# Where the softmax's normalisation runs, and how the first branch's keys are made

## The chip, the cores and the metric

The kernel runs on one core of one Trainium2 chip. The metric is the device time of one execution in microseconds (us); lower is better. TensorE (PE), VectorE (DVE), ScalarE (ACT), GpSimd (POOL) and SyncE (SP, which starts the weight transfers) each run their own instruction list in order, and wait for one another by semaphores. "PEld" in the profile is TensorE's loading of stationary operands, which overlaps its matmuls.

## The reference, cut to what matters

Two layers of a block with three attention branches over 512 image tokens (x) and 256 context tokens (c), width 1024, one batch. In each layer the normalised and modulated tokens `h` are projected by one wide matrix `w_in`. The first branch (`mla`) has 8 heads of 64 + 32 rotary dimensions, whose keys and values come from a 256-wide latent and whose queries come from a 384-wide latent; the rotary part of the key is shared by all heads. The second (`swa`) looks at a window of 128 tokens on either side and at the context, with a sink logit; the third (`ax`) is dense with normalised keys and queries.

```python
ckv, kr, sk, sv, ak, av = _split(p, KV_SPLITS)
kv_m = (rmsnorm(ckv, lw['mla_kv_norm']) @ lw['mla_w_ukv']).reshape(B, T, 8, 64 + 64)
k_m = concatenate([kv_m[..., :64], broadcast_to(k_rope, (B, T, 8, 32))], axis=-1)
q_m = (rmsnorm(cq, lw['mla_q_norm']) @ lw['mla_w_uq']).reshape(B, T, 8, 1, 64 + 32)
s = einsum('bqhgd,bkhd->bhgqk', q, k) * scale      # each branch
p = softmax(s);  o = einsum('bhgqk,bkhd->bqhgd', p, v)
y_b = (o_b * silu(z_b)) @ w_o_b;   y = sum_b sigmoid(g_b) * y_b;   x = x + gate * (y @ w_out)
```

In the first layer the context tokens are updated too (they have queries); in the second only the image tokens are.

## The kernel before, in words

**Precision.** Every fp32 operand of a large matmul is held as two reduced parts, high and low (`_hi`, `_lo`), and a product is three matmuls: high by high, high by low, low by high. Weights arrive by DMA in chunks of up to 128x1024 in one of a few slots; ScalarE makes the high part (`w_hi`, line 1355) and GpSimd the low one (`w_lo`, line 1528).

**Attention units.** A unit is one head by one tile of 128 query tokens; there are 48 per branch in the first layer (8 heads by 6 tiles), 32 in the second, 240 in all. Two units of one head make a pass. For each unit the function `attention` writes out, in this order, the events of every engine:

- PV: TensorE multiplies the probabilities transposed in the iteration before by the values (lines 1224 and 1225).
- T: TensorE transposes blocks of normalised exponentials `e` into `ptp` (line 1211); ScalarE copies them out as the high part (1445). They belong to a pass whose last unit is at least two units back, and TensorE waits for that unit's normalisation (`norm_done`, in the branch `ev == "T"` of TensorE's list).
- SB: TensorE's last scores of this unit into `wide` (1195), after waiting for the exponential of the unit before.
- N: VectorE normalises the exponentials of the unit *before*: a reciprocal of the sum (1731), then a multiplication of the whole 128 x width tile by it, in place (1732). The two are chained by a semaphore.
- X: VectorE's row maximum over the scores (1715) and the bias from it (1721, in `swa` 1718).
- OC, TL, O: ScalarE copies half of a finished pass's output (1454); VectorE makes the low part of the transposed probabilities (1737), adds the output's halves (1744) and gates them (1750).
- M: ScalarE's exponential with accumulated sum (1436).
- SA: TensorE's first scores of the next unit, and after it `fill`: steps of other work (projections of later heads and branches, gates, output projections) from a queue.

`fill` gives every unit an equal share of the work still listed for the branch, by the planner's costs; a credit that finds no eligible work is cut to 900 ns. Items marked urgent come first once their condition holds. The items of the first branch are `mla_head(1)` to `mla_head(7)`, the first table, keys and queries of the second branch, two gate tiles (`z`) and `values_s` (the values of the second and third branches, three groups of 48 matmuls of 256 columns, line 677).

**First branch's heads.** `mla_head(h)` (line 595) makes the keys of head h (`km`, 64 rows, six matmuls for x and six for c), on even h the values of two heads (`vm`), and the queries of head h+1 (`qm`); head 0 makes the queries of heads 0 and 1. A head's work may start when head h-2 has been issued, since `k_m` has two buffers. The rotary rows of the keys (`kr`) are written into both buffers once a layer. The weights of one `mla_head` form one chunk `mk`.

**Memory.** `k_m` is two buffers in one tensor; `v_s` (values of the later branches) lies at offset 12288 to 24576 of the shared area, `lat_r` and `ak_sq` at 18432 and 21504.

Of the kernel before, what the change touches and what calls it, by code (L numbers as in the profile page):

```python
# [122 lines left out]
def schedule():  # L123
# [416 lines left out]
    for l in range(LAYERS):  # L540
# [52 lines left out]
        first_q = {0: (0, 1), 7: ()}  # L593

        def mla_head(h):

            qs = first_q.get(h, (h + 1,))
            c = chunk("mk", l, h, qs)
            kg = [project("km", l, c, tg, src="ckv", m=MLA_NOPE, width=MLA_NOPE, k=KKV, needs=lambda: latents, what="km", head=h)
                  for tg in ("x", "c")]  # L600
            ready.setdefault(("mla", h), []).extend(kg)
            vg = []
            if h % 2 == 0:
                vg = [group("vm", chunk_ids=(c,), mode="vm", l=l, cost=cost_of(128, 6 * 3), co=KKV * MLA_NOPE,
                            tts=range(tt, tt + 3), what="vm", pair=h // 2, needs=lambda: latents) for tt in range(0, TT, 3)]
                ready_v["mla", h // 2] = vg
            qg, co = [], KKV * (MLA_NOPE + 2 * MLA_V * (h % 2 == 0))
            for i, hq in enumerate(qs):
                got = [project("qm", l, c, tg, src="cq", co=co + i * KQ * MLA_K, m=MLA_K, width=MLA_K, k=KQ,
                               needs=lambda: latents, what="qm", head=hq, **roped(tg)) for tg in tgs]  # L610
                ready.setdefault(("mla", hq), []).extend(got)
                qg += got
            return [s for g in (qg + kg + vg if h == 0 else kg + qg + vg) for s in g["steps"]]
# [32 lines left out]
        def q_pair(branch, t):  # L646
            def make():
                c = chunk("win", l, C_Q[branch] + t * P, P)
                gs = [project("qs", l, c, tg, what="qs", head=2 * t, branch=branch,
                              kx=keys[branch][0]["low_n"], **roped(tg, squares=branch == "ax")) for tg in tgs]  # L650
# [18 lines left out]
        for h in range(1, HEADS):  # L669
            cost = cost_of(SEQ, 9 + 6) + cost_of(CTX, 6 + 9 * (len(tgs) > 1)) + (2 * cost_of(128, 18) if h % 2 == 0 else 0)  # L670
            item(("mla", h), "mla", cost, lambda s, h=h: h < 2 or ("mla", h - 2) in s, lambda h=h: mla_head(h), urgent=True)
# [5 lines left out]
        item("values_s", "mla", 3 * cost_of(256, 48), lambda s: True, values_s)  # L677
# [70 lines left out]
def build(nc, t_in, out):  # L748
# [62 lines left out]
    k_m = shared("k_m", [P, 2, 2, TOK], R, 63488)  # L811
# [44 lines left out]
    with ExitStack() as stack:  # L856
# [26 lines left out]
        s_done, max_done, exp_done, norm_done = (semaphore(k) for k in ("s_done", "max_done", "exp_done", "norm_done"))  # L883
        pt_done, pt_hi_ready, pt_lo_ready = semaphore("pt_done"), semaphore("pt_hi_ready"), semaphore("pt_lo_ready")
# [24 lines left out]
        def f(ap):  # L909
            return ap.bitcast(F)  # L910


        def chunk_dma(c):
# [18 lines left out]
            if kind == "mk":  # L932
                h, qs = chunks[c][2:]
                got, at = [], KKV * MLA_NOPE
                got.append((raw[:, 0:at].rearrange("p (k c) -> p k c", k=KKV),
                            t_in["mla_w_ukv"][l, :, h * P:h * P + MLA_NOPE].rearrange("(k p) c -> p k c", p=P)))
                if h % 2 == 0:
                    for k in range(KKV):
                        rows = t_in["mla_w_ukv"][l, k * P:(k + 1) * P, h * P:(h + 2) * P].rearrange("p (h a d) -> p h a d", h=2, a=2)
                        got.append((raw[:, at:at + 2 * MLA_V].rearrange("p (h d) -> p h d", h=2), rows[:, :, 1, :]))  # L940
                        at += 2 * MLA_V
                for hq in qs:
                    got.append((raw[:, at:at + KQ * MLA_K].rearrange("p (k c) -> p k c", k=KQ),
                                t_in["mla_w_uq"][l, :, hq * MLA_K:(hq + 1) * MLA_K].rearrange("(k p) c -> p k c", p=P)))
                    at += KQ * MLA_K
                return got
# [5 lines left out]
        def chunk_size(c):  # L952
            kind = chunks[c][0]
            if kind == "win":
                return KD * chunks[c][3]
            if kind == "mk":
                h, qs = chunks[c][2:]
                return KKV * (MLA_NOPE + 2 * MLA_V * (h % 2 == 0)) + KQ * MLA_K * len(qs)
            return KO * P if kind == "wo" else CHUNK
# [38 lines left out]

        def q_of(u):
            cs_ = slice(u["tt"] * P, (u["tt"] + 1) * P)  # L1000
            if u["branch"] == "mla":
                return [q_m[u["h"] % 3][0:MLA_K, i, cs_] for i in range(2)]
            return [q_s[:, u["h"] % 4, cs_]]

        def k_of(u, k0, nk):
            if u["branch"] == "mla":
                return [k_m[0:MLA_K, u["h"] % 2, i, k0:k0 + nk] for i in range(2)]
            return [k_s[:, u["h"] // (HEADS // KVH), i, k0:k0 + nk] for i in range(2)]
# [100 lines left out]
        def _(pe):  # L1109
# [11 lines left out]
            for e in events:  # L1121
# [78 lines left out]
                elif ev == "T":  # L1200
                    t = e["t"]
                    if new(norm_done, t["pa"]["units"][-1]["n"] + 1):
                        pe.wait_ge(norm_done, t["pa"]["units"][-1]["n"] + 1)
# [39 lines left out]
        def pieces(g):  # L1243
# [13 lines left out]
            if what == "km":  # L1257
                s = g["head"] % 2
                return [(k_m[0:MLA_NOPE, s, 0, c], k_m[0:MLA_NOPE, s, 1, c], src[0:MLA_NOPE, 0:N])], None
            if what == "kr":  # L1260
                rows = slice(MLA_NOPE, MLA_K)
                s = src[rows, 0:N] if g["roped"] else src[0:MLA_ROPE, 0:N]
                return [(k_m[rows, i, 0, c], k_m[rows, i, 1, c], s) for i in range(2)], None
# [70 lines left out]
        def _(act):  # L1334
# [13 lines left out]
            for e in events:  # L1348
# [73 lines left out]
                elif ev == "M":  # L1422
# [10 lines left out]
                    else:  # L1433
# [3 lines left out]
                                         bias=nbias[:, r:r + 1], scale=scale, accum_out=esum[:, r:r + 1]).then_inc(exp_done, 1)  # L1437
                elif ev == "T":
# [60 lines left out]
                elif ev == "XM":  # L1499
# [4 lines left out]
                    nc.scalar.activation(h_hi[:, :, tt * P:(tt + 1) * P], m, ACT.Copy).then_inc(x_h, 1)  # L1504
                elif ev == "XS":
# [64 lines left out]
        def _(dve):  # L1570
# [30 lines left out]
            for e in events:  # L1601
# [120 lines left out]
                elif ev == "N":  # L1722
# [128 lines left out]
```

## Time and profile before

| what | us |
|---|---|
| three runs | 2092.71, 2095.66, 2084.99 (median 2092.71) |
| the profiled execution: its own time | 2090.13 |
| its span in the trace | 2088.3 |
| mean granted TensorE clock | 0.947 of full speed |

The page gives each engine's busy time, the costliest groups of instructions and the chain of work that ended last. In the trace, the first layer attends from about 213 to 945 us and the second from about 1350 to 1935 us; the branches follow one another, `mla`, `swa`, `ax`, with borders near 450 and 690, and near 1535 and 1730. Before, between and after lie the modulation, the latent projections and the merge and output projections. A matmul's duration in the profile is longer than the distance between two of them, because they are pipelined; distances are read from start to start. The chain of waits is followed back only to about 1280 us, so it describes the second layer's attention and end.

### The profile page before, as it was taken

The numbers are of one execution on the slowest core, as the hardware profiler recorded it, in microseconds if no ns is written. First come the engines' busy times: TensorE is split into PE (matmuls) and PEld (weight loads), VectorE is DVE, ScalarE is ACT, GpSimd is POOL, SyncE is SP. The second block draws the span as 40 slices with busy tenths as digits, with TensorE's granted clock in tenths as the row PEclk, the third lists the DMA queues.
The fourth block names the chain that finished last, engine by engine and source line by source line (L and its number), as shares of the span: only waits on it lengthen the run. The fifth ranks groups of instructions, "written<-read, shape, count | busy, mean of one in ns | idle before, by whom it ended". The sixth has DMA issues, their size and how long they took to land. (4 is left out here: it accounts for less than half of the span.)

```text
span 2088.3 us, 27530 instructions
## 1 busy us (share of the span) xinstructions
PE 1822.0 (87%) x10845; PEld 1560.1 (75%) x10845; DVE 1216.3 (58%) x2322; ACT 902.2 (43%) x1691; POOL 604.3 (29%) x328
## 2 busy tenths in 40 slices
PE   5598999879999899998888978888879988999887
PEld 2376778768998788887766966777767876878667
DVE  1524775786666677765232354376867677677324
ACT  1323554544554555544222143344545455554332
POOL 0332221212221222213455153221213323332551
PEclk9699999999999999999998989899989999999999
DMA  6220010101121111113334212110102221111442
GB/s 221 58 58 20 22 32 19 41 11 41 46 56 41 32 40 46 31 42 115 107 113 144 62 61 63 35 28 23 41 16 62 63 64 45 52 52 50 136 141 81
DMA packets 192287, 125.90 MB, mean 60 GB/s; under 512 B 21468, under 2 KB 187934, under 8 KB 192158
## 3 DMA queue, kind: packets, MB, share of 16 engines
q1 hardware_dynamic: 187248, 108.57, 18.3%
q10 hardware_dynamic: 3630, 11.37, 1.5%
q0 software_dynamic: 1280, 4.20, 0.6%
q8 instruction: 86, 1.41, 0.3%
q14 instruction: 43, 0.35, 0.1%
HBM read 119.92 MB, written 4.19 MB: 59 GB/s over the span
## 5 line engine op out<-in xcount | busy, mean ns | idle before, releaser
L1528 POOL TENSOR_TENSOR w_lo<-w_raw,w_hi 128x1024 fp32r<-128x1024 f32 (+6 forms) x220 | 464.4, 2119 | 1181.1 <-ACT w_hi L1355 1181.0
L1172 PE MATMUL acc<-h_hi,w_hi 128*128 128x512 f32 (+2 forms) x1288 | 471.2, 366 | 48.8 <-POOL w_lo L1528 24.4
L1172 PE MATMUL acc<-h_hi,w_lo 128*128 128x512 f32 (+2 forms) x1288 | 466.3, 362 | 0.0
L1172 PE MATMUL acc<-h_lo,w_hi 128*128 128x512 f32 (+2 forms) x1288 | 461.0, 360 | 0.0
L1172 PEld LDWEIGHTS acc<-h_hi,w_hi 128*128 128x128 f32 (+1 forms) x1288 | 248.9, 193 | 91.2 <-issue 27.1
L1445 ACT ACTIVATE pt<-ptp 128x512 fp32r<-128x512 f32 (+3 forms) x312 | 166.2, 563 | 280.1 <-PE ptp L1211 279.3
L1172 PEld LDWEIGHTS acc<-h_hi,w_lo 128*128 128x128 f32 (+1 forms) x1288 | 248.3, 193 | 36.6
L1172 PEld LDWEIGHTS acc<-h_lo,w_hi 128*128 128x128 f32 (+1 forms) x1288 | 246.0, 191 | 36.7
L1715 DVE TENSOR_REDUCE nmax<-wide 128x1 f32<-128x768 f32 (+3 forms) x240 | 190.5, 794 | 112.0 <-PE wide L1195 110.5
L1355 ACT ACTIVATE w_hi<-w_raw 128x1024 fp32r<-128x1024 f32 (+6 forms) x220 | 200.0, 921 | 79.6 <-DMA w_raw<-in_w_out 68.2
L1436 ACT ACTIVATE e<-wide,nbias,rq 128x768 f32<-128x768 f32 x160 | 145.1, 907 | 182.6 <-DVE nbias L1721 182.1
L1737 DVE TENSOR_TENSOR pt<-ptp,pt 128x512 fp32r<-128x512 f32 (+3 forms) x312 | 192.1, 641 | 40.2 <-ACT pt L1445 40.2
L1732 DVE TENSOR_SCALAR e<-e,einv 128x768 f32<-128x768 f32 (+3 forms) x240 | 176.3, 735 | 8.5
L1211 PE MATMUL ptp<-ident,e 128*128 128x128 f32 x1152 | 168.5, 281 | 0.0
L1195 PE MATMUL wide<-k_s,q_s 128*128 128x256 f32 (+2 forms) x576 | 128.1, 340 | 16.9 <-DVE q_s L1313 11.1
L1211 PEld LDWEIGHTS ptp<-ident,e 128*128 128x128 f32 x1152 | 136.5, 145 | 1.4
L1224 PE MATMUL pv<-pt,v_s 128*128 128x256 f32 (+1 forms) x384 | 100.8, 289 | 36.9 <-DVE pt L1737 22.5
L1224 PEld LDWEIGHTS pv<-pt,v_s 128*128 128x128 f32 x384 | 73.1, 190 | 52.0 <-DVE pt L1737 47.4
L1670 DVE SCALAR_TENSOR_TENSOR th_x<-th_x,acc 128x512 f32<-128x512 f32 x32 | 22.0, 686 | 153.4 <-PE acc L1172 153.2
L1172 PE MATMUL acc<-og_hi,w_hi 128*128 128x512 f32 (+1 forms) x288 | 103.8, 360 | 5.2 <-ACT th_x L1395 4.9
L1554 POOL TENSOR_TENSOR swapped<-swapped,sin 128x512 f32<-128x512 f32 (+2 forms) x38 | 49.8, 1309 | 188.5 <-DVE rot L1628 171.8
L1172 PE MATMUL acc<-og_hi,w_lo 128*128 128x512 f32 (+1 forms) x288 | 103.5, 360 | 0.0
(192 smaller groups left out, 3377.6 us busy)
## 6 DMA issues: line engine op xcount, KB each, us to landing
w_raw<-in_w_in SPq DMA_DIRECT2D x102, 512.0 KB, 3.8
w_raw<-in_ada_w SPq DMA_DIRECT2D x48, 512.0 KB, 3.8
w_raw<-in_w_out SPq DMA_DIRECT2D x16, 512.0 KB, 4.0
xres<-in_x ACTq DMA_DIRECT2D x2, 2048.0 KB, 9.1
w_raw<-in_w_o_mla SPq DMA_DIRECT2D x16, 256.0 KB, 2.8
w_raw<-in_w_o_swa SPq DMA_DIRECT2D x16, 256.0 KB, 2.8
w_raw<-in_w_o_ax SPq DMA_DIRECT2D x16, 256.0 KB, 2.8
w_raw<-in_mla_w_uq SPq DMA_DIRECT2D x16, 144.0 KB, 2.4
```

What stands on the lines that cost most here:

```text
L1172: ins = nc.tensor.matmul(dst, lhs, rhs, start=first, stop=last)
L1195: ins = nc.tensor.matmul(wide[:, c0:c0 + nk], lhs, rhs, start=(i == 0), stop=(i == len(pairs) - 1 and not masks))
L1211: ins = nc.tensor.transpose(ptp_of(t)[:, b:b + P], e_of(u, c0, c0 + P), ident[:, :])
L1224: nc.tensor.matmul(dst, v_of(pa, kt), pt_of(t, 0)[:, b], start=t["first"] and i == 0, stop=False)
L1355: nc.scalar.activation(w_hi[s][:, 0:k], w_raw[s][:, 0:k], ACT.Copy).then_inc(w_hi_ready, 1)
L1436: nc.scalar.activation(e_of(u), wide[:, u["lo"]:u["lo"] + u["width"]], ACT.Exp, bias=nbias[:, r:r + 1], scale=scale, accum_out=esum[:, r:r ...
L1445: nc.scalar.activation(pt_of(t, 0), ptp_of(t), ACT.Copy).then_inc(pt_hi_ready, 1)
L1528: nc.gpsimd.tensor_tensor(w_lo[s][:, 0:k], w_raw[s][:, 0:k], f(w_hi[s][:, 0:k]), ALU.subtract).then_inc(w_lo_ready, 1)
L1554: nc.gpsimd.tensor_tensor(swapped[rows, :], swapped[rows, :], sin[rows, :], ALU.mult).then_inc(rope_link, 1)
L1715: link(nc.vector.tensor_reduce(nmax[:, r:r + 1], wide[:, u["lo"]:u["lo"] + u["width"]], AX.X, ALU.max, negate=True))
L1732: nc.vector.tensor_scalar(e_of(u), e_of(u), einv[:, r:r + 1], None, ALU.mult).then_inc(norm_done, 1)
L1737: nc.vector.tensor_tensor(pt_of(t, 1), ptp_of(t), f(pt_of(t, 0)), ALU.subtract).then_inc(pt_lo_ready, 1)
```

## The change

Two parts.

1. The multiplication of N moves from VectorE to ScalarE for all three branches (`on_act = BRANCHES`): VectorE keeps the reciprocal, which signals `inv_done`; ScalarE waits for it, scales `e` in place (a Copy with a per-partition scale) and signals `norm_act`, for which the transposes wait. In ScalarE's list this stands where the event N stands: behind the copies of T, ahead of OC and of the exponential M.
2. The keys of two heads are made by one projection of 128 rows (`m` and `width` at their default 128), on even h, with a chunk `mk` that holds the keys and values of two heads and one head's queries; the other heads' queries have a chunk `mq` of their own. Odd `mla_head` makes queries only, head 7 nothing. `k_m` becomes three buffers; the third lies at 18432 and its rotary rows are copied by ScalarE once a layer (event KC, after a wait for all low parts). Since it overlaps `v_s`, `values_s` may start only when head 5 has been issued.

```diff
+        emit("KC", l_done=n["l"])
+
+        def head_q(h, c, co):
+            got = [project("qm", l, c, tg, src="cq", co=co, m=MLA_K, width=MLA_K, k=KQ,
+                           needs=lambda: latents, what="qm", head=h, **roped(tg)) for tg in tgs]
+            ready.setdefault(("mla", h), []).extend(got)
+            return got
 
         def mla_head(h):
-            qs = first_q.get(h, (h + 1,))
-            c = chunk("mk", l, h, qs)
-            kg = [project("km", l, c, tg, src="ckv", m=MLA_NOPE, width=MLA_NOPE, k=KKV, needs=lambda: latents, what="km", head=h)
-                  for tg in ("x", "c")]
...
+            kg, vg, qg = [], [], []
             if h % 2 == 0:
+                c = chunk("mk", l, h, h + 1 if h else 0)
+                kg = [project("km", l, c, tg, src="ckv", k=KKV, needs=lambda: latents, what="km", head=h) for tg in ("x", "c")]
+                for hk in (h, h + 1):
+                    ready.setdefault(("mla", hk), []).extend(kg)
...
+                qg = head_q(h + 1 if h else 0, c, KKV * 2 * (MLA_NOPE + MLA_V))
+            if h == 0 or h % 2 and h + 1 < HEADS:
+                qg += head_q(h + 1, chunk("mq", l, h + 1), 0)
             return [s for g in (qg + kg + vg if h == 0 else kg + qg + vg) for s in g["steps"]]
...
-        item("values_s", "mla", 3 * cost_of(256, 48), lambda s: True, values_s)
+        item("values_s", "mla", 3 * cost_of(256, 48), lambda s: ("mla", 5) in s, values_s)
...
-    k_m = shared("k_m", [P, 2, 2, TOK], R, 63488)
+    k_m = [shared(f"k_m{i}", [P, 2, TOK], R, at) for i, at in enumerate((63488, 69632, 18432))]
...
@@ TensorE, before a transpose
+                    if u["branch"] in on_act:
+                        if new(norm_act, invs[u["n"]]):
+                            pe.wait_ge(norm_act, invs[u["n"]])
...
@@ pieces(g), the key projection's read-out
             if what == "km":
-                s = g["head"] % 2
-                return [(k_m[0:MLA_NOPE, s, 0, c], k_m[0:MLA_NOPE, s, 1, c], src[0:MLA_NOPE, 0:N])], None
+                out_ = []
+                for i in range(2):
+                    k = k_m[(g["head"] + i) % 3]
+                    out_.append((k[0:MLA_NOPE, 0, c], k[0:MLA_NOPE, 1, c], src[i * MLA_NOPE:(i + 1) * MLA_NOPE, 0:N]))
+                return out_, None
...
@@ ScalarE
+                elif ev == "N" and e["u"]["branch"] in on_act:
+                    u = e["u"]
+                    if new(inv_done, invs[u["n"]]):
+                        act.wait_ge(inv_done, invs[u["n"]])
+                    r = u["n"] % 8
+                    nc.scalar.activation(e_of(u), e_of(u), ACT.Copy, scale=einv[:, r:r + 1]).then_inc(norm_act, 1)
...
+                elif ev == "KC":
+                    if new(l_done, e["l_done"]):
+                        act.wait_ge(l_done, e["l_done"])
+                    nc.scalar.activation(k_m[2][MLA_NOPE:MLA_K, :, :], f(k_m[0][MLA_NOPE:MLA_K, :, :]), ACT.Copy)
@@ VectorE, event N
+                    if u["branch"] in on_act:
+                        nc.vector.reciprocal(einv[:, r:r + 1], total[:, r:r + 1]).then_inc(inv_done, 1)
+                        continue
```

## Rows read from the trace of the kernel before

**Rows 1.** The page, busy time and share of the span of each engine.
```profile
PE 1822.0 (87%) x10845; PEld 1560.1 (75%) x10845; DVE 1216.3 (58%) x2322; ACT 902.2 (43%) x1691; POOL 604.3 (29%) x328
```

**Rows 2.** Busy by stretch: bounds, length, PE, PEld, DVE, ACT, POOL, granted clock, DMA.
```profile
213.00:450.00 237.00, 205.44 (x1314) 179.58 (x1314) 173.94 (x366) 116.76 (x237) 48.95 (x32) 0.93 0.10 27
450.00:690.00 240.00, 228.34 (x1460) 207.51 (x1459) 163.89 (x397) 121.38 (x292) 53.06 (x30) 0.98 0.16 43
690.00:930.00 240.00, 228.11 (x1434) 202.95 (x1435) 169.56 (x331) 126.05 (x235) 54.59 (x30) 0.99 0.15 39
...
1350.00:1535.00 185.00, 153.25 (x982) 133.41 (x981) 135.04 (x250) 88.81 (x167) 43.31 (x29) 0.94 0.11 30
1535.00:1730.00 195.00, 176.50 (x966) 153.69 (x965) 134.24 (x278) 96.67 (x211) 56.57 (x32) 0.95 0.19 52
1730.00:1935.00 205.00, 185.22 (x1035) 158.35 (x1036) 144.26 (x263) 113.96 (x195) 59.55 (x30) 0.99 0.19 51
```

**Rows 3.** The chain by line, shares of the stretch: 1350:1535, 1535:1730, 1730:1935.
```profile
by line: PE acc L1172 17.6%; DVE nmax L1715 10.3%; DVE e L1732 10.0%; issue 6.4%; PE wide L1195 6.4%; DVE pt L1737 6.0%; PE ptp L1211 4.9%; ACT e L1436 4.1%; PE pv L1224 3.4%; DVE q_m L1313 2.8%; PE pv L1225 2.6%; DVE k_s L1313 2.4%; DVE nb
...
by line: PE acc L1172 35.1%; PE ptp L1211 7.1%; PE wide L1195 6.6%; DVE nmax L1715 4.9%; PE pv L1224 4.6%; DVE e L1732 4.0%; PE pv L1225 4.0%; DVE pt L1737 3.8%; issue 3.8%; DVE k_s L1313 3.5%; DVE q_s L1313 2.7%; ACT q_s L1304 1.7%; ACT k_
...
by line: PE acc L1172 36.8%; PE ptp L1211 7.2%; PE wide L1195 6.5%; PE pv L1224 5.2%; DVE nmax L1715 4.5%; PE pv L1225 4.2%; DVE e L1732 4.2%; DVE pt L1737 4.0%; POOL w_lo L1528 3.5%; issue 3.4%; DVE q_s L1313 1.9%; DVE y L1673 1.9%; ACT e 
```

**Rows 4.** The chain in time, 1439 to 1441 us: start, length, engine and line.
```profile
1439.49 0.62 DVE e L1732
1440.11 0.88 DVE nmax L1715
```

**Rows 5.** Waits over the span: who waited for whom, total us, times, longest.
```profile
DVE nmax L1715 <- PE wide L1195: 110.5, 84, 3.8
PE pv L1224 <- DVE pt L1737: 39.3, 36, 3.7
PE pv L1224 <- DVE o_half L1744: 36.3, 27, 3.9
ACT e L1436 <- DVE nbias L1721: 182.1, 133, 4.3
```

**Rows 6.** Groups by form, line 1732: count | busy us, mean ns | idle before.
```profile
L1732 DVE TENSOR_SCALAR e<-e,einv 128x768 f32<-128x768 f32 x128 | 110.3, 862 | 4.5
...
L1732 DVE TENSOR_SCALAR e<-e,einv 128x256 f32<-128x256 f32 x48 | 25.5, 532 | 1.7
...
L1732 DVE TENSOR_SCALAR e<-e,einv 128x640 f32<-128x640 f32 x32 | 22.9, 716 | 1.1
...
L1732 DVE TENSOR_SCALAR e<-e,einv 128x512 f32<-128x512 f32 x32 | 17.5, 548 | 1.1
```

**Rows 7.** Groups by form, two ScalarE instructions near the added one in shape.
```profile
L1436 ACT ACTIVATE e<-wide,nbias,rq 128x768 f32<-128x768 f32 x128 | 127.0, 992 | 164.8 <-DVE nbias L1721 164.6
...
L1498 ACT ACTIVATE xn<-xres,rstd 128x1024 f32<-128x1024 f32 x12 | 13.7, 1138 | 22.1 <-DVE rstd L1771 22.1
```

**Rows 8.** Timeline, 1449 to 1451 us: start, length, engine, line.
```profile
1449.47 1.27 POOL L1554 TENSOR_TENSOR swapped<-swapped,sin 96x512 f32<-96x512 f32 x1 [1.84 <-DVE rot L1628]
1449.49 1.66 DVE L1732 TENSOR_SCALAR e<-e,einv 128x768 f32<-128x768 f32 x1
```

**Rows 9.** Groups by form: one third of the key matmuls, their read-out on VectorE.
```profile
L1172 PE MATMUL acc<-ckv_hi,w_hi 128*64 128x512 f32 x32 | 13.4, 419 | 6.8 <-POOL w_lo L1528 4.6 <-DVE rot L1628 2.2
...
L1313 DVE TENSOR_TENSOR k_m<-acc,k_m 64x512 fp32r<-64x512 f32 x16 | 10.9, 682 | 20.3 <-ACT k_m L1304 17.3 <-PE acc L1172 2.9
```

**Rows 10.** Timeline of key matmuls at full clock, 389.0 to 389.5 us.
```profile
389.07 0.40 PE L1172 MATMUL acc<-ckv_lo,w_hi 128*64 128x512 f32 x1
389.30 0.28 PE L1172 MATMUL acc<-ckv_hi,w_hi 128*64 128x256 f32 x1
389.42 0.28 PE L1172 MATMUL acc<-ckv_hi,w_lo 128*64 128x256 f32 x1
```

**Rows 11.** Groups by form: one third of the matmuls of `values_s`, both layers.
```profile
L1172 PE MATMUL acc<-w_hi,h_hi 128*128 128x256 f32 x96 | 27.5, 286 | 0.0
```

More of the change, by code:

```diff
@@ L649, in make @@
                 gs = [project("qs", l, c, tg, what="qs", head=2 * t, branch=branch,
-                              kx=keys[branch][0]["low_n"], **roped(tg, squares=branch == "ax")) for tg in tgs]
+                              kx=keys[branch][0].get("low_n", 0), **roped(tg, squares=branch == "ax")) for tg in tgs]
                 got = list(gs)
@@ L932, in chunk_dma @@
             if kind == "mk":
[L933 to L937, printed above, removed]
+                h, hq = chunks[c][2:]
+                got, at = [], 0
+                for a in range(2):
                     for k in range(KKV):
                         rows = t_in["mla_w_ukv"][l, k * P:(k + 1) * P, h * P:(h + 2) * P].rearrange("p (h a d) -> p h a d", h=2, a=2)
[L940 to L946, printed above, removed]
+                        got.append((raw[:, at:at + P].rearrange("p (h d) -> p h d", h=2), rows[:, :, a, :]))
+                        at += P
+                return got + [(raw[:, at:at + KQ * MLA_K].rearrange("p (k c) -> p k c", k=KQ),
+                               t_in["mla_w_uq"][l, :, hq * MLA_K:(hq + 1) * MLA_K].rearrange("(k p) c -> p k c", p=P))]
+            if kind == "mq":
+                hq = chunks[c][2]
+                return [(raw[:, 0:KQ * MLA_K].rearrange("p (k c) -> p k c", k=KQ),
+                         t_in["mla_w_uq"][l, :, hq * MLA_K:(hq + 1) * MLA_K].rearrange("(k p) c -> p k c", p=P))]
             b, t = chunks[c][2:]
@@ L956, in chunk_size @@
             if kind == "mk":
-                h, qs = chunks[c][2:]
-                return KKV * (MLA_NOPE + 2 * MLA_V * (h % 2 == 0)) + KQ * MLA_K * len(qs)
+                return KKV * 2 * (MLA_NOPE + MLA_V) + KQ * MLA_K
+            if kind == "mq":
+                return KQ * MLA_K
             return KO * P if kind == "wo" else CHUNK
@@ L996, in _ @@
                     sp.wait_ge(out_saved[i], 16 * (TT - TT_CTX) // 2)
+        on_act, invs, norms = BRANCHES, {}, {}
+        for e_ in events:
+            if e_["ev"] == "N":
+                counts = invs if e_["u"]["branch"] in on_act else norms
+                counts[e_["u"]["n"]] = len(counts) + 1
         def q_of(u):
@@ L1006, in k_of @@
             if u["branch"] == "mla":
-                return [k_m[0:MLA_K, u["h"] % 2, i, k0:k0 + nk] for i in range(2)]
+                return [k_m[u["h"] % 3][0:MLA_K, i, k0:k0 + nk] for i in range(2)]
             return [k_s[:, u["h"] // (HEADS // KVH), i, k0:k0 + nk] for i in range(2)]
@@ L1262, in pieces @@
                 s = src[rows, 0:N] if g["roped"] else src[0:MLA_ROPE, 0:N]
-                return [(k_m[rows, i, 0, c], k_m[rows, i, 1, c], s) for i in range(2)], None
+                return [(k_m[i][rows, 0, c], k_m[i][rows, 1, c], s) for i in range(2)], None
             if what == "og":
```

21 lines of the change are left out of this document (8 added, 13 removed).

## The prediction, made before the changed kernel was run

> **What bounds the kernel now.** First the page: TensorE is busy 87% of the span, VectorE 58%, ScalarE 43% [rows 1]. A mean over stages hides where VectorE matters, so the second view is the busy time by stretch [rows 2]. In the two stretches of the first branch TensorE is idle 31.6 us (237.0 less 205.4) and 31.7 us (185.0 less 153.3), its granted clock is 0.93 and 0.94, and VectorE is busy 73% of both. In the other four it is idle 11.7, 11.9, 18.5 and 19.8 us and the clock is 0.95 to 0.99. So attention holds 125 us of idle TensorE, half of it in the first branch; the rest is TensorE's own throughput.
>
> Third, the chain of waits, which the profile could follow back only through the second layer [rows 3]. In the first branch VectorE's maximum and its scaling of the exponentials are the largest entries behind the projections, 10.3% and 10.0%; in the other two the scaling has 4.0% and 4.2%. In order of time the reader sees how it gets there: the scaling ends at 1440.11 and the next unit's maximum starts at 1440.11 [rows 4]. The scores were there; the maximum stood behind the scaling in VectorE's list. Over the span VectorE waited for scores ahead of only 84 of 240 maxima [rows 5], so in most units it came late. Late maxima delay the low parts behind them, and TensorE waits for these and for the output's sum, 39.3 and 36.3 us [rows 5].
>
> **The change part by part.**
>
> *The scaling leaves VectorE.* It removes 240 instructions, 110.3 + 25.5 + 22.9 + 17.5 = 176 us [rows 6]. The reciprocal stays. What can come off the end is what lies on the chain: 10.0% of 185, 4.0% of 195 and 4.2% of 205 us are 18.5 + 7.8 + 8.6 = 34.9 us in the second layer; the first has no chain, and the same shares of its stretches (237, 240, 240) give 23.7 + 9.6 + 10.1 = 43.4. The upper end is 78 us; in no stretch does it exceed TensorE's idle time. The lower end is 0, if TensorE was about to be late anyway. I take 45%, 35 us: what is late next is TensorE's in-order list (transposes, scores and projections make a third of that chain in the first branch and over half in the others), and the 84 units that waited for scores gain nothing.
>
> *It arrives on ScalarE.* The trace has no scaled copy of this width. Above lies the exponential of the same width, 0.99 us, with one operand more and its source in another memory; below, the scaled copy of 1024 columns, 1.138 us, shrunk in proportion to 0.85 [rows 7]. Between ends this close I take 0.92. For all widths I scale VectorE's 176 us by 0.92/0.862, which gives 188 us (174 to 203); ScalarE goes from 902 to about 1090 us, and from 49% to about 63% in the first branch's first stretch. Does it reach the path? The instruction added waits for the reciprocal, and queued behind it are the copy of the output half and the exponential; for them wait the output's sum and the next scores. But the exponential can't start until VectorE, after that same reciprocal, has done the maximum (0.88 here) and the bias, so 0.92 us of scaling has about 1.1 us of cover, provided that the copies of the transposes in front of it are done. ScalarE stood idle ahead of 133 of 160 exponentials of the first and third branch, 1.37 us in the mean [rows 5]. The lower end is therefore 0. The upper end: the 27 without idle time pay 0.92 each, 25 us, over all 240 units 37 us. I take 5 us, near the lower end because cover and scaling have the same trigger. The transposes that wait for the result belong to a unit two back, and the scaling stands ahead of an exponential that TensorE's scores wait for anyway: nothing, 0 to 5 us.
>
> A page speaks against this part. The Trainium skill, "ScalarE: Activation LUTs", section "What ACT_TABLE_LOAD costs", says that ScalarE takes one element per lane and cycle at 1.2 GHz plus about 280 ns with one pointer operand, an estimate of 0.92 us for 768 columns, where an undisturbed VectorE took 0.62 [rows 4]. So the work itself gets longer by 0.3 us a unit and only its place can pay. On the other side the scaling took 1.66 us beside a GpSimd instruction of 1.27 us that had started 0.02 us earlier [rows 8], against 0.62 alone. The Trainium skill, "SBUF — State Buffer", section "SBUF: two separate sides", says that GpSimd and a two-port VectorE instruction take one port pair by an exclusive lock, and ScalarE has ports of its own; a blocked 0.62 would then end 1.89 us after it started, the trace has 1.66, so the order of size agrees. It changes no term: the mean of 0.862 [rows 6] holds that loss already.
>
> *Keys two heads at a time.* The key projections have 32 matmuls of 512 columns of each of three kinds [rows 9], 96, and as many of 256 columns. Half go: 48 at 0.23 us from start to start and 48 at 0.12 [rows 10], 11.0 + 5.8 = 16.8 us of TensorE. Bounds 0 and 17. The first branch is not limited by TensorE alone, so I take 60%, 10 us.
>
> *Read-out of the keys.* The number of copies stays, but two now follow one matmul group, so its accumulator bank is freed 0.68 us later per engine [rows 9], up to 1.4 us in 8 groups of 512 columns: 0 to 11 us, less because half as many groups are read out. I take 2.
>
> *Values held back until head 5 is issued.* 288 matmuls of 0.12 us [rows 10, 11] are 17 us a layer that used to be filler in the middle of the branch. Before head 5 the eligible filler is now the heads and two gate tiles, and it can run out; afterwards keys, queries and values crowd into the last two heads. Where filler is missing, a unit takes the time of its own chain. Work is moved, not added: lower end 0. Upper end: about ten units a layer, each 1 us emptier, 20 us. I take 5, since the units behind head 5 were the emptier ones before.
>
> *Small parts.* The third buffer's rotary rows are one ScalarE copy of 1536 columns per layer, about 1.7 us in proportion to the 1.138 of [rows 7], beside TensorE's first query projection, which doesn't need ScalarE for its image tokens: 0, or 3.4 if the cover fails. It waits for low parts for which TensorE waits too. Transfers per layer are 24 before (5, 2, 4, 2, 4, 2, 4, 1) and 24 after (four of 5, four of 1), the chunks 8 and 8, the columns split by ScalarE and GpSimd 4352 and 4352: the queues of SP and GpSimd keep their load. At the branch's start a second small chunk must be split, behind nine matmul triples that cover it: 0 to 1 us.
>
> Sum: -35 - 10 + 5 + 2 + 5 = -33 us. The profiled execution took 2090.1 us, its span 2088.3; that gives 2057. The median of the runs lies 2.6 us above it, so I predict 2060 us.
>
> **Rivals.** A difference under about 0.5%, 10 us, can't be told from no change here.
>
> *A, the relief is taken back by TensorE.* TensorE's list is in order and 87% busy; if it was only just behind VectorE, shorter maxima end in an earlier wait for the same projections, and the keys' 17 us fall into idle time. For it: four of six stretches have TensorE at 90% or more. Against: 64 us idle in the first branch. A tenth of the 78 us and a third of the 17 less the 12 of added costs is about 2 us: 2091.
>
> *B, ScalarE becomes the late one: slower.* In ScalarE's list the scaling stands behind the copies of the transposes. If these end late, as when both tiles of a pass come together (two copies of 0.6 us and the half output), cover is gone and exponential, scores and maximum all shift. For it: the instruction is longer than the one removed, and it is ahead of the most critical one on its engine. Against: the 1.37 us of idle. With half of the relief and of the keys' gain (39 + 8) and 7 us of the small losses, it decides from (47 - 7)/240 = 0.17 us exposed per unit; at 0.3 us it costs 72, and 72 - 47 + 7 = +32 on the 2093 of before gives 2125; at 0.22 us, 53 - 47 + 7 = +13, 2106.
>
> *C, the whole chain share comes off.* 78 + 17 less 12 is 83 us: 2010. For it, VectorE at 73% with the waits of 76 us for it; the granted clock of 0.93 could rise to the 0.98 of the other stretches, which is 5% of 390 us, some 15 us that the sum leaves out. Against: every other path would need that much slack. A half-way case lies near 2035.
>
> *D, the values' gap.* Filler runs out and the forced waits for rotary queries show as idle TensorE before head 5: 20 us a layer in place of 5 in both, 2095.
>
> **How the numbers follow.** Forecast (2040 to 2082) 0.50, C and half-way 0.17, A and D together 0.20, B 0.13. Faster by over 0.5% (under 2082) is the first two, 0.67; within 0.5% 0.20; slower 0.13. The range leaves out the far end of C and of B: 2022 to 2100.
>
> **What would show it.** Right: VectorE near 1040 us and ScalarE near 1090; matmuls fewer by 96; the maximum preceded by waits for scores in far more than 84 units; TensorE's waits for the low parts and the output's sum well under 76 us; the first branch's stretches shorter by some 12 us each, the others by 2 to 5. The step on ScalarE is wrong if the exponential, now waiting for nothing, has scaling directly in front of it on the chain. The whole is wrong if the stretches of the first branch keep their 237 and 185 us, or if idle TensorE before head 5 eats them.

## The result, and the profile after

The changed kernel takes 2023.2 us (median of 4 runs, 2020.6 to 2025.8) against 2093.0 for the one before: ratio 0.967, interval 0.964 to 0.970, or -70 us. The forecast was 2060. The sign was right and the time lies in the range, but the gain is over twice the -33 forecast. Of all the executions in this document one stands apart and is left out: one of e15's five took 2584 us, at a mean granted clock of 0.642.

The page of the changed kernel, to be read against [rows 1]:

```profile
span 2024.0 us, 27323 instructions
...
PE 1794.5 (89%) x10749; PEld 1547.1 (76%) x10749; DVE 1048.1 (52%) x2082; ACT 1075.1 (53%) x1933; POOL 599.1 (30%) x328
```

VectorE and ScalarE came out where the forecast had them (1040 and 1090), and the matmuls are 96 fewer. The added instruction, by form, answers to [rows 6] (count | busy us, mean ns | idle before):

```profile
L1461 ACT ACTIVATE e<-e,einv 128x768 f32<-128x768 f32 x128 | 119.5, 934 | 30.9 <-DVE einv L1760 30.6
...
L1461 ACT ACTIVATE e<-e,einv 128x256 f32<-128x256 f32 x48 | 24.3, 506 | 3.2 <-DVE einv L1760 3.1
```

The widest takes 0.934 us where 0.92 was taken; all four widths together take 193 us where 188 were taken. So the sizes of the instructions were right. Where the time went is read from the stretches between fixed points, each from the first scores of a branch to the first scores of what follows. Before (bounds, length, PE, PEld, DVE, ACT, POOL, granted clock, DMA; the rows are the first branch and the other two, for each layer):

```profile
213.30:447.90 234.60, 203.03 (x1303) 177.18 (x1301) 173.52 (x365) 116.76 (x237) 48.65 (x32) 0.94 0.11 28
447.90:952.20 504.30, 480.74 (x3044) 432.52 (x3045) 348.96 (x758) 257.59 (x545) 111.74 (x62) 0.98 0.15 41
1336.70:1534.70 198.00, 166.20 (x1048) 143.11 (x1046) 142.41 (x265) 94.99 (x178) 49.85 (x32) 0.95 0.12 32
1534.70:1920.70 386.00, 352.70 (x1943) 304.41 (x1944) 270.16 (x525) 205.29 (x395) 115.77 (x62) 0.97 0.19 52
```

And the changed kernel:

```profile
216.30:416.00 199.70, 180.40 (x1231) 161.48 (x1229) 139.30 (x310) 144.29 (x274) 45.00 (x30) 0.99 0.11 27
416.00:910.60 494.60, 480.42 (x3069) 433.31 (x3068) 293.08 (x668) 321.98 (x647) 114.79 (x63) 0.99 0.16 43
1294.30:1471.10 176.80, 151.77 (x968) 134.19 (x967) 110.13 (x224) 116.45 (x201) 46.68 (x31) 0.95 0.12 30
1471.10:1853.90 382.80, 355.44 (x1977) 307.67 (x1976) 222.88 (x468) 256.59 (x465) 115.86 (x63) 0.97 0.21 56
```

The first branch is shorter by 34.9 and 21.2 us, the other two together by 9.7 and 3.2; what lies outside attention is within 5 us in sum. The first branch also hands 25 and 34 matmuls of filler to the others, which still got shorter. Stretches are from one execution each and carry some noise: e12 below has the very instructions of the changed kernel in the second layer, and its first branch there took 180.6 us for 176.8, at a granted clock of 0.93 for 0.95. The chain over its stretch in the second layer answers to the first row of [rows 3]:

```profile
by line: PE acc L1183 30.1%; PE wide L1206 10.9%; PE ptp L1226 9.3%; PE pv L1239 6.8%; DVE nmax L1743 6.5%; PE pv L1240 5.5%; issue 3.7%; DVE pt L1768 3.6%; ACT e L1454 3.3%; POOL w_lo L1556 2.7%; DVE k_m L1331 2.6%; ACT w_hi L1373 2.3%; AC
```

The scaling is gone from it on either engine, the maximum fell from 10.3% to 6.5%, and TensorE's own lines are about 63% where they were 35%. The waits answer to [rows 5]:

```profile
DVE nmax L1743 <- PE wide L1206: 206.0, 133, 7.1
...
ACT e L1461 <- DVE einv L1760: 46.8, 53, 2.8
...
PE pv L1239 <- DVE pt L1768: 29.6, 25, 3.1
...
ACT e L1454 <- DVE nbias L1749: 24.6, 47, 2.3
PE pv L1239 <- DVE o_half L1775: 24.0, 16, 2.5
```

VectorE now waits for the scores ahead of 133 maxima, not 84. TensorE's two waits for VectorE fell from 75.6 to 53.6 us. ScalarE's idle time ahead of the exponential fell from 182 to 25 us, and 47 us of idle are new ahead of the scaling itself: the scaling sits where ScalarE had waited for the bias, as the cover argument said, and has used most of that room up.

### The profile page after: what moved, and what is told of

Same layout as the page of the kernel before. It is cut to its first block and busy times, and to the rows that moved or that the text cites. A ratio compares the mean times of both kernels' runs of the same rounds, so it can differ in the third digit from the quotient of the medians.

```text
span 2024.0 us, 27323 instructions
## 1 busy us (share of the span) xinstructions
PE 1794.5 (89%) x10749; PEld 1547.1 (76%) x10749; DVE 1048.1 (52%) x2082; ACT 1075.1 (53%) x1933; POOL 599.1 (30%) x328
## 5 line engine op out<-in xcount | busy, mean ns | idle before, releaser
L1556 POOL TENSOR_TENSOR w_lo<-w_raw,w_hi 128x1024 fp32r<-128x1024 f32 (+3 forms) x220 | 462.7, 2111 | 1160.0 <-ACT w_hi L1373 1159.6
L1373 ACT ACTIVATE w_hi<-w_raw 128x1024 fp32r<-128x1024 f32 (+3 forms) x220 | 199.6, 921 | 76.1 <-DMA w_raw<-in_w_out 66.9
L1461 ACT ACTIVATE e<-e,einv 128x768 f32<-128x768 f32 (+3 forms) x240 | 193.3, 805 | 47.4 <-DVE einv L1760 46.8
L1413 ACT ACTIVATE th_x<-acc 128x512 f32<-128x512 f32 x72 | 42.7, 593 | 138.2 <-PE acc L1183 138.1
L1183 PE MATMUL acc<-og_lo,w_hi 128*128 128x512 f32 (+1 forms) x288 | 103.1, 358 | 0.0
```

Source lines behind the costliest of these rows:

```text
L1183: ins = nc.tensor.matmul(dst, lhs, rhs, start=first, stop=last)
L1373: nc.scalar.activation(w_hi[s][:, 0:k], w_raw[s][:, 0:k], ACT.Copy).then_inc(w_hi_ready, 1)
L1413: ins = nc.scalar.activation(th[g["tg"]][:, :], src[:, 0:N], ACT.Tanh, scale=0.5)
L1461: nc.scalar.activation(e_of(u), e_of(u), ACT.Copy, scale=einv[:, r:r + 1]).then_inc(norm_act, 1)
L1556: nc.gpsimd.tensor_tensor(w_lo[s][:, 0:k], w_raw[s][:, 0:k], f(w_hi[s][:, 0:k]), ALU.subtract).then_inc(w_lo_ready, 1)
```

## The experiments

All ratios are to the kernel before on the same chip, with 95% intervals. Times in us are medians; where two runs are compared across chips, the ratios are the better measure.

**Taking the two parts apart.** e1 is the kernel before with only the scaling moved. e2 is the changed kernel with the scaling left on VectorE, so it keeps only the keys' part:

```diff
-        on_act, invs, norms = BRANCHES, {}, {}
+        on_act, invs, norms = (), {}, {}      # e2, on the changed kernel
```

> The kernel before with only the scaling moved to ScalarE; keys, chunks and values as before. Both changes together gave -70 us. Theory S (the scaling leaving VectorE takes nearly its whole chain share off): 2093 - 55 = 2038 us or less, the first branch's stretches shorter by some 28 and 14 us. Theory K (most of what the forecast missed comes from how keys, queries and values are now arranged): about 2093 - 30 = 2063 us, as the forecast had it for this part alone.

Measured: 2041.6 us, ratio 0.978 (0.975 to 0.981), -46 us.

> The changed kernel with the scaling left on VectorE: keys two heads at a time, third buffer, values held back. Theory S: the keys give 10 us or less, 2083 us or above. Theory K: 2063 to 2053 us. If the two parts need each other (each alone leaves the other as the next late one), this run and the one with the scaling alone fall short of -70 us in sum by 15 us or more.

Measured: 2079.1 us, 0.995 (0.994 to 0.997), -10 us. The scaling gives 46 where the forecast had 30 (35 less 5 for ScalarE); the keys alone give 10, and on top of the moved scaling about 22 by the ratios (0.967 against 0.978; 18 by the medians), where the forecast had 3. Together the ratios give 68, so the parts reinforce each other by some 12 us; the three intervals together leave 9 us either way, and the 15 set for a clear sign isn't reached. Neither theory has it all: theory S named the larger part, at 46 instead of 55, and about half of the missing 37 us is in the keys.

The stretches of e1 (the first branch of each layer) and of e2 (first branch, other two, for each layer):

```profile
212.20:429.30 217.10, 192.52 (x1302) 169.69 (x1301) 141.85 (x318) 148.91 (x284) 47.25 (x32) 0.98 0.12 30
...
1305.10:1490.40 185.30, 161.55 (x1047) 140.15 (x1046) 114.65 (x234) 121.32 (x209) 48.16 (x32) 0.97 0.14 35
```
```profile
221.00:440.00 219.00, 189.86 (x1230) 168.78 (x1229) 172.88 (x357) 110.93 (x228) 47.05 (x30) 0.95 0.10 25
440.00:946.70 506.70, 483.42 (x3071) 434.85 (x3070) 354.01 (x763) 261.48 (x552) 114.16 (x63) 0.98 0.16 42
...
1327.80:1520.00 192.20, 162.81 (x967) 144.36 (x966) 137.46 (x255) 91.52 (x171) 49.24 (x31) 0.89 0.11 28
1520.00:1912.70 392.70, 358.77 (x1977) 309.81 (x1976) 274.01 (x532) 208.91 (x402) 118.34 (x63) 0.96 0.21 54
```

In the first branch of the first layer the two parts simply add: -17.5 and -15.6, together -34.9. Where they don't add is mostly the other two branches. With the keys' part alone these take over filler and get 2.4 and 6.7 us longer; with the scaling moved they take over the same filler and still get shorter (-9.7 and -3.2). e2 also starts its first scores 7.7 us later than the kernel before (221.0 for 213.3), which eats a good part of its gain in the first branch.

One thing changes with the waits that the sum had left out: TensorE's granted clock. In e1 TensorE's matmuls in the first branch are those of the kernel before, to a missing record, and yet its busy time there fell by 10.5 and 4.7 us (203.03 to 192.52, 166.20 to 161.55), with a granted clock of 0.98 for 0.94 and 0.97 for 0.95. That is half of the 30.2 us by which these two stretches got shorter; the other half is less idle time. How much of it is cause and how much consequence of the shorter waits, no run separates.

**Is it VectorE's time?** e4 puts a useless maximum where the scaling was:

```diff
                         nc.vector.reciprocal(einv[:, r:r + 1], total[:, r:r + 1]).then_inc(inv_done, 1)
+                        nc.vector.tensor_reduce(spare[:, r:r + 1], f(h_hi[:, 0, 0:u["width"]]), AX.X, ALU.max)
```

> The changed kernel with a row maximum over as many columns of the high part of h, its result unused, put into VectorE's list where the scaling stood, so that VectorE is as full as before while ScalarE still does the scaling. Theory S (VectorE's time is what counted): back up by 45 to 60 us, 2068 to 2083 us, about the keys-only time. If instead the distance from the exponential to the transposes counted, it stays within 15 us of 2023.

Measured: 2068.5 us, 0.991 (0.988 to 0.993), 45 us back. The filling in the trace:

```profile
L1762 DVE TENSOR_REDUCE spare<-h_hi 128x1 f32<-128x768 f32 x128 | 119.2, 931 | 0.0
```

All widths together hold VectorE for 185 us, where the scaling had held it for 176. In the changed kernel the move of the scaling is worth 56 us (2079.1 less 2023.2), and 45 of them are lost again, though ScalarE still does the scaling. So the gain is in the main VectorE's time in its list; 24% of the time put in reaches the end. Here too the clock goes along: in the first branch the same 1231 and 968 matmuls keep TensorE busy for 7.0 and 9.0 us more than in the changed kernel, at 0.96 for 0.99 and 0.90 for 0.95, out of 14.8 and 11.9 us by which the stretches got longer:

```profile
217.60:432.10 214.50, 187.43 (x1231) 166.32 (x1229) 168.82 (x357) 144.39 (x274) 44.88 (x30) 0.96 0.10 25
...
1316.30:1505.00 188.70, 160.74 (x968) 142.19 (x967) 136.00 (x255) 116.90 (x201) 46.65 (x31) 0.90 0.11 28
```

**ScalarE's share of the bill.** e7 cuts each scaling into four pieces:

```diff
-                    nc.scalar.activation(e_of(u), e_of(u), ACT.Copy, scale=einv[:, r:r + 1]).then_inc(norm_act, 1)
+                    quarter = u["width"] // 4
+                    for i in range(4):
+                        part = e_of(u, i * quarter, (i + 1) * quarter)
+                        ins = nc.scalar.activation(part, part, ACT.Copy, scale=einv[:, r:r + 1])
+                    ins.then_inc(norm_act, 1)
```

> The changed kernel with each scaling on ScalarE cut into four pieces, which lengthens ScalarE's list by about 4 x 0.4 - 0.9 = 0.7 to 0.9 us a unit and adds nothing elsewhere. Cover theory (the scaling hides under maximum and bias, some 1.1 us): the first 0.2 us are covered, the rest, 0.5 to 0.7 us a unit, is partly exposed: +30 to +80 us. If ScalarE has wide slack: +10 or less.

Measured: 2060.3 us, 0.986 (0.982 to 0.989): +37 us. ScalarE's busy time rose from 1075.1 to

```profile
PE 1814.7 (88%) x10749; PEld 1562.0 (76%) x10749; DVE 1038.3 (50%) x2082; ACT 1197.9 (58%) x2653; POOL 599.0 (29%) x328
```

1197.9, by 0.51 us a unit, and 30% of it reaches the end: in the changed kernel time added to ScalarE is about as dear as time added to VectorE. Rival B's mechanism is real and shows at 0.51 us more per unit; where below that it begins was not tested.

e12 tries the balance from the other side: the 48 units of context tokens are scaled by VectorE again (`e_["u"]["tt"] >= TT_CTX` in place of the test on the branch, in the lists of TensorE, ScalarE and VectorE), 20 us off ScalarE's busy time and 22 us onto VectorE's. Before the run, 2015 us was expected if ScalarE's time now hurt more, 2030 if VectorE's. Measured: 2028.9 us, 0.970 (0.968 to 0.972). That is 6 us above the changed kernel, with intervals that overlap: no gain is to be had this way, and the run doesn't tell more.

e8 asks whether the scaling should stand ahead of the copies:

```diff
+            if 0 < i <= len(units):
+                emit("N", u=units[i - 1])
             for t in valued:
                 T(t)
             if u:
                 SB(u)
-            if 0 < i <= len(units):
-                emit("N", u=units[i - 1])
```

> The changed kernel with the normalisation's event put ahead of the transposes in the written order, so that ScalarE scales before it copies the transposed tiles, and VectorE's order stays the same. If the place behind the copies exposes part of the scaling (the cost the forecast set at 5 us): 2018 to 2013 us. If the copies, which now come later, are what TensorE waits for: slower, 2030 or more. If both are covered: 2023.

Measured: 2042.8 us, 0.977 (0.973 to 0.981): 20 us slower than the changed kernel. Who waited, in e8:

```profile
ACT e L1461 <- DVE einv L1760: 224.3, 169, 6.1
...
PE pv L1239 <- DVE pt L1768: 39.8, 30, 3.4
```

ScalarE now blocks on the reciprocal 169 times, the copies stand behind it, and TensorE's wait for the low parts made from them rises from 29.6 to 39.8 us. The place behind the copies is the right one.

**Which branches.** e6 scales on ScalarE in the first branch only (`on_act = ("mla",)`).

> The changed kernel with ScalarE scaling in the first branch only; the other two scale on VectorE as before. The theory that the relief pays where VectorE is fullest: most of the difference between keys only (2079) and the changed kernel (2023) is kept, 2035 to 2042 us. If relief pays in proportion to the scaling removed (64 + 16 of 240 units' work in the first branch, about a third): 2060.

Measured: 2050.2 us, 0.981 (0.977 to 0.985). The move gives 29 us in the first branch and 27 in the two others; neither expectation fits, and the time lies half-way between them. The other two branches hold two thirds of the units (160 of 240) and took half of the gain. That is the split which the forecast's chain shares had (36 of 78 us), so a unit in the first branch gains about twice what one in the others does.

**What in the keys' part pays.** Not TensorE's work. e5 issues the key matmuls twice, e9 (on the kernel with only the scaling moved) leaves out half of them and with them half of the sum over the latent:

```diff
-                run(a[0:g["m"], 0:size(g["tg"])], pairs)
+                for _ in range(2 if g["kind"] == "km" else 1):      # e5
+                    run(a[0:g["m"], 0:size(g["tg"])], pairs)
...
+                if g["kind"] == "km":                               # e9
+                    pairs = pairs[:3]
```

> The changed kernel, with every matmul of the key projections issued twice (the second series overwrites the first with the same sums). TensorE gets back the 48 + 48 matmuls that the change removed, 16.8 us, and nothing else changes. If TensorE's time now counts in full (with VectorE relieved it is the next late one): 2023 + 17 = 2040 us. If the 60% of the forecast holds: 2033. If the gain of the key part lies in the order of filler and in the buffers instead: 2026 or less.

Measured: 2020.3 us, 0.967 (0.963 to 0.970): 96 matmuls more leave the time where it was. They are not all swallowed by idle time, though. Attention as a whole took 5.0 us longer than in the changed kernel (1258.9 for 1253.9, one execution of each), the rest 10.1 us less, at a higher granted clock: the mean over the span is 0.957 to 0.958 in e5's runs and 0.950 to 0.953 in the changed kernel's. Between the layers, for instance, e5 took 376.4 us where the changed kernel took 383.7:

```profile
911.70:1288.10 376.40, 323.87 (x1954) 273.47 (x1953) 144.33 (x215) 121.57 (x177) 155.17 (x77) 0.93 0.30 92
```
```profile
910.60:1294.30 383.70, 330.68 (x1941) 279.45 (x1940) 149.21 (x215) 121.53 (x177) 155.14 (x77) 0.91 0.29 90
```

> The scaling moved to ScalarE, keys organised as before, but of each key projection only the first three of six matmuls are issued (half of the sum over the latent is left out). TensorE does 96 matmuls fewer, as with the paired keys, while order, read-outs and buffers stay. If TensorE's time is what the key part gave: 2042 - 17 = 2025 us. If, as doubling them in the changed kernel suggests, it counts for almost nothing: 2038 to 2044, and the 20 us between the scaling alone and both parts come from the arrangement.

Measured: 2048.9 us, 0.980 (0.977 to 0.982), beside 0.978 with all of them: 96 fewer give nothing, and here the mean granted clock is lower (0.942 to 0.947, for 0.947 to 0.954 in e1).

Not the held values either, nor the number of accumulator groups, nor the third buffer. e3 and e10 hold the values back, in the kernel before and in e1; e11 makes the two heads' keys by two projections of 64 rows again; e14 is e10 with three key buffers (e3, e10 and e14 also take over the change's edit by which a query projection may be planned before the keys' low part):

```diff
...
-        item("values_s", "mla", 3 * cost_of(256, 48), lambda s: True, values_s)
+        item("values_s", "mla", 3 * cost_of(256, 48), lambda s: ("mla", 5) in s, values_s)   # e3, e10
...
+                kg = []
+                for hk in (h, h + 1):                                                        # e11
+                    own = [project("km", l, c, tg, src="ckv", co=(hk - h) * MLA_NOPE, m=MLA_NOPE, k=KKV, needs=lambda: latents,
+                                   what="km", head=hk) for tg in ("x", "c")]
...
```

> The kernel before with only one edit: the values of the later branches may start only when head 5 has been issued. The forecast charged 5 us for it: 2098 us. If it leaves gaps before head 5: up to 2113. If it helps, because a 17 us block of filler no longer stands in front of the next head's keys (work once begun is finished first): under 2088 us, and then it is part of what the forecast missed.

Measured: 2087.0 us, 0.999 (0.997 to 1.000): no loss of 5 us; the interval reaches no change.

> The scaling moved to ScalarE, keys as before, and the values held back until head 5 is issued. If holding them is what the key part gives once VectorE is relieved: 2030 us or less. If it is worth the 3 us that it gave alone: 2038 to 2041.

Measured: 2039.5 us, 0.975 (0.972 to 0.978): 2 us less than e1 by the medians and 6 by the ratios, with intervals that overlap.

> The changed kernel in all (chunks, three buffers, values held, both heads' keys made at the even head), except that the two heads' keys are again two projections of 64 rows, with as many matmuls and accumulator groups as before and the planner told of them. If order and buffers give the gain: within 5 us of 2023. If the fewer accumulator groups and the planner's smaller costs do: 2038 to 2045.

Measured: 2026.6 us, 0.969 (0.966 to 0.971), within its interval of the changed kernel.

> The scaling moved to ScalarE, values held back, keys made a head at a time in the old order from the old chunks, but into three buffers (with the copy of the rotary rows). If the third buffer as such is what the key part gives: 2025 us or less. If it is where the odd heads' keys stand in the order: 2038 to 2042, as without it.

Measured: 2037.8 us, 0.975 (0.973 to 0.978), as e10.

Two things are left between e10 and e11, 13 us with equal matmuls and groups and the values held in both: the order, and the chunks in which the weights arrive. e11 has the new ones (`mk` and `mq`), e14 still the old. As to the order, in e11, as in the changed kernel, an odd head's keys are made with those of the even head before it. Before, every head border could force the next head's keys, with everything queued in front of them. The last exponential of head 4 and the first of head 5 in the first layer, kernel before:

```profile
343.81 0.56 ACT L1436 ACTIVATE e<-wide,nbias,rq 128x256 f32<-128x256 f32 x1
364.33 0.99 ACT L1436 ACTIVATE e<-wide,nbias,rq 128x768 f32<-128x768 f32 x1 [1.01 <-DVE nbias L1721]
```
```profile
344.00:364.00 20.00, 14.87 (x79) 11.14 (x78) 6.86 (x15) 5.35 (x12) 4.49 (x4) 0.83 0.19 47
```

For 20.5 us no unit starts. TensorE ends the values' projection (to 345.4 us) and runs the next item as a whole, head 5's keys and with them the queries of the head after (to 351.6). Then the planner needs still more work before head 5's keys have been read out, and takes head 6's keys, whose weights aren't ready: 4.6 of the 5 us of idle are a wait for the low part of these weights. The granted clock is 0.83 over the 20 us, and 0.50, the lower of TensorE's two levels (1.2 GHz), in the 4 us after that wait:

```profile
356.35 0.69 PE L1172 MATMUL acc<-ckv_hi,w_hi 128*64 128x512 f32 x1 [4.58 <-POOL w_lo L1528]
```
```profile
351.50:356.30 4.80, 0.27 (x3) 0.04 (x1) 0.98 (x2) 1.23 (x3) 4.08 (x4) 0.74 0.41 109
356.30:360.30 4.00, 3.95 (x10) 2.44 (x11) 0.00 (x0) 0.00 (x0) 0.41 (x1) 0.50 0.00 0
```

The changed kernel there:

```profile
332.65 0.56 ACT L1454 ACTIVATE e<-wide,nbias,rq 128x256 f32<-128x256 f32 x1
341.09 0.99 ACT L1454 ACTIVATE e<-wide,nbias,rq 128x768 f32<-128x768 f32 x1 [0.61 <-DVE nbias L1749]
```

8.4 us. Holding the values also removes that gap (19.8 us in e1, 7.1 in e10), and still that layer's stretch only fell from 217.1 to 214.6 us: one long gap is not worth its length, since its work has to go somewhere. In e10 the borders to heads 6 and 7 are 8.4 and 6.1 us and one unit inside head 6 takes 9.4 us; with the odd keys ready (changed kernel) they are 5.9, 4.6 and 6.6. The seven borders of the first layer sum to 40.1 us in e10 and 34.2 in e11, those of the second to 50.5 and 44.4 (in the changed kernel 35.0 and 49.6). That the order is the cause is thus argued, from these gaps and by exclusion; no run moved the odd keys alone, and none kept the order with the old chunks. As everywhere the clock goes along: 0.94 in e10's first stretch, 0.97 in e11's.

**A better version.** The units of heads 4 and 5 have hardly any filler once the values are held. e13 reckons the share before head 5 from what may run by then:

```diff
+            if branch == "mla" and ("mla", 5) not in issued:
+                rest -= sum(q["cost"] for q in queue if q["name"] in ("values_s", "keys_s", ("swa", 0)))
+                left -= 2 * len(token_tiles(l))
```

> The changed kernel, but before head 5 is issued the share of filler per unit is reckoned only from the filler that may run by then and the units until then. Same instructions; the 6 to 9 units per layer of heads 4 and 5 that have almost no filler share what others had. If thin units take the time of their own chain (3.2 to 3.8 us in the first layer, 4.2 in the second) and crowded ones TensorE's, spreading saves up to 10 to 20 us: 2003 to 2013. If the order of filler doesn't count: 2023. If the first heads get later by it and stall: above 2028.

Measured: 2011.8 us, 0.962 (0.960 to 0.965). e15 is the changed kernel beside it:

> The changed kernel itself, on the same chip as these: 2020 to 2026 us by every theory.

Measured: 2024.7 us, 0.969 (0.966 to 0.971). So e13 beats both kernels, by 13 us over the changed one. Its first-branch stretches:

```profile
215.80:420.50 204.70, 185.27 (x1230) 164.33 (x1229) 138.11 (x310) 144.84 (x274) 45.22 (x30) 0.97 0.10 26
...
1294.90:1454.50 159.60, 148.18 (x968) 130.46 (x967) 107.49 (x224) 116.52 (x201) 46.81 (x31) 0.99 0.13 33
```

The second layer's fell from 176.8 to 159.6 us with the same instructions, while the first layer's rose from 199.7 to 204.7. The granted clock moved the same way, from 0.95 to 0.99 and from 0.99 to 0.97, but TensorE's busy time accounts for only 3.6 of the 17.2 us in the second layer and for nearly all of the 5.0 in the first. Spreading pays in the second layer only; why the first doesn't follow is open.

## Why the prediction was off

- *What bounds the kernel.* Right: VectorE's list, in which the maximum stood behind the scaling, with the first branch as the densest place. e4 and e6 show it.
- *The scaling leaves VectorE*, "I take 45%, 35 us": the mechanism was right and the term mis-sized. With the 5 us for ScalarE it was to give 30 net; e1 measured 46, which is 59% of the chain's 78 us even after ScalarE's costs. The discount rested on TensorE being late next. e5 and e9 show that 17 us of TensorE's work more or less leave the time where it was, so TensorE's lateness was worth less than the discount.
- *The clock*, left out of the sum and named only in case C (5% of 390 us is 19.5, not the 15 given there): it belongs in it. In e1 TensorE's busy time in the first branch fell by 15.2 us with the same matmuls, and over the span by 9.9 (1822.05 to 1812.17). This is of the size of what the term for the scaling lacked, 16 us.
- *It arrives on ScalarE.* Right in size (0.934 us) and in its cover; of 182 us of idle 25 are left, and 47 ahead of the scaling. e7 and e8 show how thin it is. (In the working on [rows 8] a blocked scaling would end 1.87 us after its start, not 1.89, as it started 0.02 us later; nothing hangs on it.)
- *Keys two heads at a time*, "I take 60%, 10 us": failed in its reason. The 96 matmuls saved are worth nothing (e5, e9). With its side costs the whole part was to give 3 us; it gives 10 alone and about 22 beside the moved scaling. What pays in its place the working had at nothing: the arrangement, that is, when the odd heads' keys are ready and in which chunks the weights come. e11, which keeps the arrangement and undoes the saving, is 13 us faster than e10; that it is the order and not the chunks is argued, not shown.
- *Read-out of the keys*, +2: no sign of it; e11 undoes the pairing and gains nothing. *Values held back*, +5: measured -3 (e3) and -2 to -6 (e10), neither clear of zero. *Small parts*: the first scores came 3 us later (213.3 to 216.3), as against 0 to 1 for the second chunk and nothing for the copy; in other runs with this key part it is 1.2 (e5) to 7.7 us (e2).
- *Rivals.* Case C named the price nearest to the result (2010, half-way 2035) and had 0.17. Cases A and D did not occur; B's mechanism appears at 0.5 us more per unit.
- *The sum* treated the parts as separate. Some 12 us come from both together, as far as the intervals let one say.
- *Luck.* The measured 2023 us lies in the range only because that reached down to 2022, far into case C. It is outside the band of 2040 to 2082 that the sum stood for: two of its terms were too small, both in the same direction.

## What to carry to other kernels

Where the chain of waits enters an instruction whose successor starts at the same moment, don't cut its chain share in half without a reason: here 59% came off in e1 (46 of 78 us) and 72% with the keys' part beside it (56 of 78). Price the granted clock with the waits, from stretches with equal matmuls. Before counting an engine's saved work, ask whether it is late; here doubling 96 matmuls left the time where it was. And in a planner that finishes work once begun, read the distances between units one by one, the empty as well as the crowded: a different arrangement of the same work was worth 13 us twice (e10 to e11, changed kernel to e13), 96 matmuls nothing.

## What was unexpected of the hardware

The granted clock moved with each part of the change. Its mean over the span, from the fast runs of each kernel, is 0.944 before, 0.951 with the scaling moved (e1), 0.952 with both parts and 0.958 with the key matmuls issued twice on top of that (e5). It is 0.939 with the keys' part alone (e2) and 0.940 with VectorE refilled (e4). Taking 96 matmuls away from e1 gave 0.945 (e9), so in these runs more of TensorE's work went with a higher clock and less of it with a lower one.

Adding matmuls left it no lower in the stretch itself: in the second layer's first branch it was 0.95 in the changed kernel and 0.98 with the keys issued twice, and the stretch took 176.8 and 175.3 us. In the 20 us gap shown above, where TensorE was busy 14.9 of 20 us, it was 0.83; over the whole of that stretch 0.94. After the wait of 4.6 us in that gap, matmuls of 512 columns start 0.43 us apart, where they start 0.23 us apart at full clock before it.
